# Two attentions on one core: the second product of a pair of heads issued as alternating 64-column matmuls

## What is computed

```python
# first layer, 8 heads of 64 columns, blocks of 128 queries, causal, with a forget bias
for blk in range(L // Q_BLOCK):
    q0, kend = blk * Q_BLOCK, (blk + 1) * Q_BLOCK
    s = jnp.einsum('bqhd,bkhd->bhqk', q[:, q0:kend], k[:, :kend]) * scale
    s = s + cum[:, :, q0:kend, None] - cum[:, :, None, :kend]
    s = jnp.where(k_pos[None, :] <= q_pos[:, None], s, NEG_INF)
    p = jax.nn.softmax(s, axis=-1)
    outs.append(jnp.einsum('bhqk,bkhd->bqhd', p, v[:, :kend]))

# second layer, 4 heads of 64 columns, a band of 9 chunks of 64 keys
s = jnp.einsum('bcqhd,bckhd->bchqk', qc, kb) * (HEAD_DIM ** -0.5)
p = jax.nn.softmax(jnp.where(valid, s + bias, NEG_BIG), axis=-1)
o = jnp.einsum('bchqk,bckhd->bcqhd', p, vb)

# short convolution of the first layer, beside its attention
v = gate_c * x_in
return gate_b * (vp[:, 0:L] * conv_w[0] + vp[:, 1:1 + L] * conv_w[1] + vp[:, 2:2 + L] * conv_w[2])
```

## Time and profile before

| what | value |
|---|---|
| median of 3 runs | 3498.69 us (3495.9 to 3499.28) |
| profiled execution | 3496.17 us, span 3494.5 us, 1.7 us around it |
| PE busy | 3397.4 us, 97% of the span |
| DVE, ACT, POOL busy | 39%, 27%, 26% |
| fox attention | about 310 to 792 us |
| band attention | about 1851 to 2099 us |

### The profile page before, as it was taken

How to read it: one execution, slowest core, us unless ns; L and a number is a source line. 1 busy time by engine, 2 the same in 40 slices (tenths; PEclk the granted TensorE clock), 3 DMA queues, 4 the chain that set the end, 5 groups by cost and what they waited for, 6 DMA issues and landing times. The chain is left out here.

```text
span 3494.5 us, 40873 instructions
## 1 busy us (share of the span) xinstructions
PE 3397.4 (97%) x16184; PEld 2791.9 (80%) x16184; DVE 1357.1 (39%) x1651; ACT 946.0 (27%) x1248; POOL 909.0 (26%) x450
## 2 busy tenths in 40 slices
PE   8999999999999999999999999999999999999997
PEld 6788888887877888888868887777778688888886
DVE  6843556444325121212153336554552521121123
ACT  3222434344323111111133333313342411111112
POOL 2211111112341222222422114231254222222225
PEclk9999999999999999999999999999999999999998
DMA  3535434215422111111224323223353211111113
GB/s 128 157 94 157 151 121 151 85 61 211 141 76 79 48 48 48 48 48 48 97 102 132 95 73 127 79 73 141 132 195 124 79 48 48 48 48 48 48 49 131
DMA packets 101602, 333.42 MB, mean 95 GB/s; under 512 B 11920, under 2 KB 21520, under 8 KB 101328
## 3 DMA queue, kind: packets, MB, share of 16 engines
q1 hardware_dynamic: 100432, 327.95, 28.0%
q10 hardware_dynamic: 1040, 3.67, 0.3%
HBM read 249.06 MB, written 85.52 MB: 96 GB/s over the span
## 5 line engine op out<-in xcount | busy, mean ns | idle before, releaser
L282 POOL TENSOR_TENSOR w_lo<-w_raw,w_hi 128x1024 fp32r<-128x1024 f32 (+1 forms) x304 | 698.2, 2301 | 2423.8 <-ACT w_hi L278 2423.7
L322 PE MATMUL pair<-act_hi,w_hi 128*128 128x512 f32 x2976 | 942.8, 398 | 6.6 <-DVE f1v L1957 1.5
L322 PE MATMUL pair<-act_lo,w_hi 128*128 128x512 f32 x2976 | 920.5, 391 | 0.0
L322 PE MATMUL pair<-act_hi,w_lo 128*128 128x512 f32 x2976 | 918.8, 390 | 0.0
L322 PEld LDWEIGHTS pair<-act_hi,w_lo 128*128 128x128 f32 x2976 | 559.3, 188 | 119.6
L322 PEld LDWEIGHTS pair<-act_lo,w_hi 128*128 128x128 f32 x2976 | 559.5, 188 | 119.4
L322 PEld LDWEIGHTS pair<-act_hi,w_hi 128*128 128x128 f32 x2976 | 540.3, 189 | 111.2 <-issue 9.0
L278 ACT CAST w_hi<-w_raw 128x1024 fp32r<-128x1024 f32 x274 | 287.6, 1050 | 866.5 <-PE pair L322 820.7
L609 DVE TENSOR_TENSOR p<-pair,rs 128x1024 f32<-128x1024 f32 x100 | 122.2, 1222 | 402.8 <-PE pair L322 402.7
L1900 DVE TENSOR_TENSOR f2v<-pair,rs 128x1024 f32<-128x1024 f32 x42 | 51.4, 1225 | 333.1 <-PE pair L322 333.1
L322 PE MATMUL pair<-f1hh,w_hi 128*128 128x512 f32 x480 | 147.8, 389 | 0.0
(11 more groups left out here) (478 smaller groups left out, 4065.2 us busy)
## 6 DMA issues: line engine op xcount, KB each, us to landing
w_raw<-in_stream SPq DMA_DIRECT2D x275, 512.0 KB, 3.5
proj<-p SPq DMA_DIRECT2D x101, 512.0 KB, 2.6
m2g<-proj SPq DMA_DIRECT2D x32, 512.0 KB, 4.8
m1g<-proj SPq DMA_DIRECT2D x16, 512.0 KB, 3.4
x<-f1y SPq DMA_DIRECT2D x16, 512.0 KB, 2.6
act_lo<-x SPq DMA_DIRECT2D x16, 512.0 KB, 6.6
foxx<-proj SPq DMA_DIRECT2D x28, 256.0 KB, 5.8
fx_cb<-fox_cum SPq DMA_DIRECT2D x8, 512.0 KB, 7.3
```

What stands on the lines that cost most here:

```text
L282: last = nc.gpsimd.tensor_tensor(wlo[:, slot, at:at + n], raw[:, slot, at:at + n], whi[:, slot, at:at + n].bitcast(F32), ALU.subtract)
L322: last = nc.tensor.matmul(out_pair[:, h * HALF:(h + 1) * HALF], wt, a[:, h * HALF:(h + 1) * HALF], start=k == 0 and n_pass == 0, stop=k == ...
```

## The change

`weigh` becomes `turn`. For an even head it only transposes, into a new buffer `pe` that holds the transposed probabilities of all tiles of that head (36 blocks in the fox, 30 in the band). For an odd head it transposes into `pt` and then multiplies for both heads of the pair: for each block of keys one matmul with the 64 columns of the even head's values and `pe`, into rows 0 to 63 of `bank[1]`, and one with the 64 columns of the odd head's and `pt`, into rows 64 to 127. `gather` copies all 128 rows, in odd heads only. Softmax waits for the tile's transposes (`turned`) and no longer for its product. The points of the weave are set anew: half a point more for each tile of an even head, 28 for each head on average, 235 and 124 in all.

To make room, `pt` and `o` have one slot instead of two, and `cvy` is dropped: the convolution's taps go to `cvc`, so that SP waits for the store of a row before it fetches the next.

```diff
@@ short_conv
-        y = sb(at, "cvy", [P, L])
+        y = gc
...
             if i:
                 SP.wait_ge(*convolved[i - 1])
+                SP.wait_ge(*stores[1].last())
...
-            V.mark(V.then(stores[1].last()).tensor_scalar(y[:], xin[:], w(2), None, ALU.mult))
+            V.mark(V.then().tensor_scalar(y[:], xin[:], w(2), None, ALU.mult))
@@ attention
-            s, pt = sb(at, name + "s", [P, 3, L]), sb(at, name + "pt", [P, 2, L])
-            o, st = sb(at, name + "o", [P, 2, L]), sb(at, name + "st", [P, 3, 2])
+            keys = [(k1 - k0) // P for q0, k0, k1 in tiles]
+            s, pe = sb(at, name + "s", [P, 3, L]), sb(at, name + "pe", [P, sum(keys), P])
+            pt, o, st = sb(at, name + "pt", [P, NT, P]), sb(at, name + "o", [P, L]), sb(at, name + "st", [P, 3, 2])
...
-            def weigh(t, h, n, k0, nk, e):
-
-                sl = t % 2
-                point(1 if nk > 4 else 4 if n == 0 else 1.5)
+            def turn(t, h, n, k0, nk, e):
+
+                few, even = nk <= 4, pe[:, sum(keys[:n]):sum(keys[:n + 1]), :]
+                point((1.5 if few else 1) + (2 if n == 0 else 0))
                 if t == 0:
                     PE.after(*settled)
-                state["copied"] = transposes(pt[:, sl, :].rearrange("p (j n) -> p j n", n=P),
-                                             lambda j: s[:, t % 3, j * P:(j + 1) * P], nk, P, e, free=state["copied"],
-                                             after=lambda: point(1 if nk > 4 else 1.5))
+                state["copied"] = transposes(pt[:, 0:nk, :] if h % 2 else even, lambda j: s[:, t % 3, j * P:(j + 1) * P], nk, P,
+                                             e, free=state["copied"], after=lambda: point(1.5 if few else 1))
+                turned.append(state["copied"])
+                if h % 2 == 0:
+                    point(0.5)
+                    return
                 PE.after(state["copied"], values_in[h], state["o_read"])
                 for j in range(nk):
-                    last = nc.tensor.matmul(bank[1][:, n % 4 * P:(n % 4 + 1) * P], vt[:, h // 2 % 2, k0 // P + j, :],
-                                            pt[:, sl, j * P:(j + 1) * P], start=j == 0, stop=j == nk - 1)
-                pv_done.append(PE.mark(last))
-                weighed[h] = pv_done[-1]
+                    for x, p in enumerate((even, pt)):
+                        mine = slice(x * HD, (x + 1) * HD)
+                        last = nc.tensor.matmul(bank[1][mine, n % 4 * P:(n % 4 + 1) * P], vt[:, h // 2 % 2, k0 // P + j, mine],
+                                                p[:, j, :], start=j == 0, stop=j == nk - 1)
+                pv_done[t] = weighed[h] = PE.mark(last)
...
-                if n % 4 != 3:
+                if h % 2 == 0 or n % 4 != 3:
                     return
...
-                V.after(ready, bias_ready[h], pv_done[t - 3] if t > 2 else None, *(settled if t == 2 else ()))
+                V.after(ready, bias_ready[h], turned[t - 3] if t > 2 else None, *(settled if t == 2 else ()))
@@ the weaves
-            w.again(FOX_HEADS * 26 + 11, 2 * KT)
+            w.again(FOX_HEADS * 28 + 11, 2 * KT)
...
-                w.again(BAND_HEADS * 26 + 12, 32 * KT)
+                w.again(BAND_HEADS * 28 + 12, 32 * KT)
```

More of the change, by code:

```diff
@@ L750, in values @@
                 return copied
-            pv_done, state = [], {"copied": None, "o_read": None, "scores_read": None}
+            pv_done, turned, state = {}, [], {"copied": None, "o_read": None, "scores_read": None}
             def scaled(t, h, n, k0, nk, e):
@@ L776, in gather @@
+                pv_done[t] = weighed[h] = PE.mark(last)
             def gather(t, h, n):
-                if n % 4 != 3:
+                if h % 2 == 0 or n % 4 != 3:
                     return
[L780 to L783, removed]
+                state["o_read"] = V.mark(V.after(pv_done[t], out_in.get(h // 2 - 1)).tensor_copy(
+                    o[:, n // 4 * HALF:(n // 4 + 1) * HALF], bank[1][:]))
@@ L784, in gather @@
+                if n == NT - 1:
                     SP.wait_ge(*V.last())
-                    out_in[h // 2] = stores[0].mark(SP.dma_start(mixed[h // 2 + row0], o[:, slot, :]))
+                    out_in[h // 2] = stores[0].mark(SP.dma_start(mixed[h // 2 + row0], o[:]))
             out_in = {}
@@ L811, in attention @@
                 if ready_p:
-                    weigh(*ready_p)
+                    turn(*ready_p)
                 drained = ready_p
```

## The result

The changed kernel takes 3470.05 us in the median of 4 runs (3466.54 to 3474.16), the kernel before 3498.1 us (3495.9 to 3499.28): 28 us less, ratio 0.9923, 95% interval 0.9911 to 0.9935. The profiled execution took 3470.16 us with a span of 3468.5 us, against 3496.17 and 3494.5 us.

What follows compares the result with a forecast made beforehand. PE, busy 97% of the span, bounds the kernel; product 30.7 plus weave 1.8 less late row 1.5 gives 31.0 us, from 3498.7 to 3467.7, rounded to 3468 us. Forecast range 3460 to 3476 (64%); 8 in 10: 3456 to 3483 us.

Steps and rivals of the forecast that it cites:

- The sum of 31.0 us: Whole program: product 30.7 us plus weave 1.8 us less late convolution row 1.5 us, profiled execution 3496.2 to 3465.2 us.
- The record's price: Product of probabilities and values: a half-width record in alternation costs 0.0546 us, against 0.112 us at full width.
- The switch: Product's bursts: going to the halved array and back costs 0.34 us a burst, 16.3 us for 48 bursts.
- The product's gain: Probabilities times values in both attentions: 91.6 to 60.9 us, 30.7 us gained, 22.3 in the fox, 8.4 in the band.
- The end of the fox: Last head's weave: woven tiles stand at the seventh tile and none at the eighth, 1.8 us gained.
- The convolution's row: DVE's row at an even head's end: head 3's wait grows, head 5 may get one, 1.5 us lost.
- the waits of 0.2 to 1.1 us there stay about as they are: Middle turns, where prepare loads DVE and ACT: half a point's 0.44 us replaces a product of 0.3 to 0.9 us.
- the signs named at the end of the prediction: Trace after: among others, PE idle in the fox 8 to 16 us, fox about 22 us shorter, band 8.
- The rival of waits: Shifted weave makes PE wait for DVE, giving back 10 to 15 us: 3478 to 3484 us; chance 19% (3476 to 3488).
- SP's new wait: SP stands three times for a convolution row's store, 2.6 to 5.1 us: hidden, nothing; uncovered at most 3 x 5 us.

Runs made afterwards that it cites:

- e1: Changed kernel with the product's two loops swapped, all key blocks of the even head first, then all of the odd head: 3498.12 us, ratio 1.0002.
- e2: Kernel before with each head multiplying only its own 64 columns into its own 64 rows, still in its own turns: 3521.13 us, ratio 1.0066.
- e4: Changed kernel with the products of two tiles of an odd head in one burst where they fit, 28 bursts for 48: 3469.38 us, ratio 0.9917.
- e7: e5 and, besides, a head's convolution row issued at the end of its second turn instead of the start of its first: 3448.93 us, ratio 0.9858.
- e10: Kernel before with bias first on DVE and the convolution row late, and nothing of the change: 3482.13 us, ratio 0.9954.
- e11: Changed kernel with the convolution row late and DVE's order otherwise as it was: 3466.56 us, ratio 0.9913.
- e5: Changed kernel with the bias, maximum and sign of tile t issued before the turn of tile t - 2: 3463.93 us, ratio 0.9905.
- e6: Kernel before with the same alteration of DVE's order as e5, weigh in place of turn: 3494.51 us, ratio 0.999.
- e3: Kernel before with the short convolution's edit alone, taps in cvc and SP waiting for a row's store: 3497.73 us, ratio 1.0003.

## Why the prediction was right, point by point

**The number** is closer than it earned. The sum of 31.0 us was to bring the profiled execution to 3465.2 us, and it took 3470.2: 26 us gained. The forecast of 3468 us added 2.5 us, by which the median before lay above its profiled execution; in the changed kernel the two are equal. So 3 of the 5 us by which the sum missed are hidden by luck.

**The record's price** held: 0.0546 us was taken from two other mixers, and the changed kernel shows a pair every 0.11 us. That alternation is what brings it was inferred from rows and is now shown by `e1` and `e2`.

**The switch** at 0.34 us a burst was read from one place in the hgrn mixer. The timeline of the changed kernel gives 0.35 us, differences of busy time give 0.28 to 0.29 us (`e4`, `e2`). In the sum of 48 bursts this leaves 2 to 3 us open; the lower price of a lone narrow record closes a part of it for `e2`.

**The product's gain** of 30.7 us: the direct measure is `e7` against `e10`, 31.5 us of busy time and 33.2 us of time with the 1.8 us at the fox's end in it, where the sum had 32.5 us. By stretches it is 24.6 us in the fox, told 22.3 + 1.8, and 8.9 us to the band's end, told 8.4. The medians of 4 runs that spread over 9 us leave a few us open. In the kernels as they were PE's busy time fell by 29.0 us.

**The end of the fox** came out as told; the seventh tile waits no more, the eighth does, with the waits of the earlier trace rows:

```profile
772.25 0.63 PE L638 MATMUL bank<-ident,foxs 128*128 128x128 f32 x4 [0.77 <-ACT foxpt L642]
```

**The convolution's row** was told right in its mechanism and put at 1.5 us. The wait in head 3 was told at 1.5 to 2 us and is 2.4; head 5 has one of 0.4 us; together 2.0 us more than before. Two more waits stand at head 3's start, ahead of its first scores and its second transposes. They are not the row's, since `e11` still has both with the row moved away; the first stands behind an eviction:

```profile
474.44 0.30 PE L811 MATMUL wide<-foxks,foxqh 128*128 128x128 f32 x1 [1.24 <-DVE foxs L854]
...
478.92 0.52 PE L638 MATMUL bank<-ident,foxs 128*128 128x128 f32 x3 [0.79 <-ACT foxpe L642]
483.25 0.35 PE L811 MATMUL wide<-foxks,foxqh 128*128 128x256 f32 x1 [2.42 <-DVE foxs L854]
```

**What failed** is the sentence that in the middle turns "the waits of 0.2 to 1.1 us there stay about as they are". For the waits behind `prepare` it held, 3.2 us before and 2.7 after. For those behind an eviction it did not, 1.0 us before and 7.2 after. It weighed the length of a turn, product against half a point. But what covers an eviction is what PE still has to do when a block of eight tiles ends, and there an even head no longer has its product, whatever its turn's length. That DVE's order makes these waits is shown by `e5` and `e6`; the missing product as their cause is argued from the places where they stand. Idle time of PE in the fox up to its end went from 12.3 to 16.8 us where the sum expected 12.0, and where the signs named at the end of the prediction allowed 8 to 16. This and 1.1 us less busy time gained than the 22.3 told make the fox's 16.8 us out of the 22.6 forecast; the band gave 9.3 us where 8.4 were told. The rival of waits was thus partly at work, at 4 to 5 us instead of 10 to 15 (which, added to 3467.7, would have been up to 3483 us and not 3484).

**SP's new wait** was put at nothing, and `e3` shows nothing that is clear of noise.

## What to carry to other kernels

Where a matmul uses only 64 of its 128 stationary columns and another like it exists, issue them alternately into the two halves of a bank: the pair then costs what one did, plus some 0.3 us for each burst between full-width work. Keep such bursts few and long, and alternate matmul by matmul, since in these bursts halves in turn gave it all back. When work is taken off the bottleneck engine, look at what stood last before each of its waits: work that covered another engine's in-order queue can leave a wait when it moves. Ordering that queue by who is waited for (here the bias ahead of evictions, a side job beside the longest turn) was worth 21 us in the changed kernel and 17 in the kernel before, beside the 28 us of the change.

## What the runs showed of the hardware beyond what was expected

Records for the other half of the array start past up to three records for the busy half that stand ahead of them in the program, so that halves in turn overlap at their seam: three records of each in the bursts of three and more blocks (those of one and two overlap whole), 28.1 us lost instead of the 47 expected. The Trainium skill, "TensorEngine Tiling (Array Packing)", says under "Key Properties" that different tiles can load weights and multiply in parallel; this case's trace agrees, with pairs 0.01 us apart, and bounds it by the order of the instructions.

The switch to half width and back costs 0.28 to 0.35 us between full-width matmuls, and a half-width record alone is hardly cheaper than a full one (0.109 and 0.112 us; a burst of 16 is 1.96 and 1.95 us long).

In the changed kernel DVE's small addition of the causal part, 0.29 us elsewhere, took 1.62 us at 352.90 and 1.25 us at 474.33 while POOL formed `w_lo` over 128x1024, and ended 0.14 us after POOL both times (354.38 and 475.44). In `e5` the convolution's first product, 1.22 us elsewhere, began at 409.22 and took 2.84 us, ending 1.1 us after POOL did at 410.98. DVE's addition of the bias, which reads `wide` in PSUM, took 1.21 us at 473.09 beside POOL, no more than elsewhere (1.22 to 1.23 us). So some of DVE's operations seem to stand until POOL's ends, and others not; no run here moves POOL's work to test it.
